# A two-block transformer kernel on one core: the high by high terms of each stage's first product are issued ahead of the terms with low parts

## What is computed

```python
def rmsnorm(a, g):
    af = a.astype(jnp.float32)
    af = af * lax.rsqrt(jnp.mean(af * af, axis=-1, keepdims=True) + EPS)
    return (af * g.astype(jnp.float32)).astype(a.dtype)
...
        h = rmsnorm(x, g_mix[i])
        z = h @ w_in[i]
...
        y = jnp.concatenate([rmsnorm(y_c, g_out_conv[i]), rmsnorm(y_a, g_out_attn[i])], axis=-1)
        x = x + y @ w_out[i]
        h = rmsnorm(x, g_ffn[i])
        gate = causal_dwconv3(h @ w_gate[i], ffn_conv_w[i], ffn_conv_b[i])
        x = x + (jax.nn.silu(gate) * (h @ w_up[i])) @ w_down[i]
        ple_gate = jax.nn.sigmoid(rmsnorm(x, g_ple[i]) @ w_ple_gate[i])
        x = x + ple_gate * (p[i].astype(x.dtype) @ w_ple_proj[i])
```

## Time and profile before

| | |
|---|---|
| median of three runs | 2513.19 us (2512.89 to 2514.77) |
| the profiled execution's own time | 2514.26 us |
| its span, first to last instruction | 2512.9 us |
| TensorE's matmuls busy | 2459.4 us, 98%, 11970 of them |
| VectorE, ScalarE, GpSimd busy | 1691.4, 1153.4 and 1469.0 us (67%, 46%, 58%) |
| mean granted TensorE clock | 0.999 |

### The profile page before, as it was taken

The page is one execution under the profiler, slowest core; times in us unless marked ns, Lnnn a source line. Parts: engine busy times, 40 slices in busy tenths (PEclk is TensorE's granted clock), DMA queues, the critical chain, the costliest instruction groups (busy, mean ns, idle before and its releaser), DMA issues.

```text
span 2512.9 us, 35613 instructions
## 1 busy us (share of the span) xinstructions
PE 2459.4 (98%) x11970; PEld 2039.0 (81%) x11970; DVE 1691.4 (67%) x2889; ACT 1153.4 (46%) x2207; POOL 1469.0 (58%) x1157
## 2 busy tenths in 40 slices
PE   8999999999999999999999999889999999999999
PEld 6888888887888888887877887679888888888887
DVE  5337776188988879997267888767238445445988
ACT  6336663253333335445256666586234333333442
POOL 2133324456777769997426555374346666667986
PEclk9999999999999999999999999999999999999999
DMA  4254323213322246332223122220321222227342
GB/s 160 76 182 129 114 77 130 105 59 118 114 100 101 106 168 222 118 95 88 91 74 91 61 70 80 89 85 22 151 76 63 107 108 101 101 97 267 118 159 97
DMA packets 125045, 274.67 MB, mean 109 GB/s; under 512 B 11809, under 2 KB 33601, under 8 KB 124609
## 3 DMA queue, kind: packets, MB, share of 16 engines
q1 hardware_dynamic: 124864, 272.40, 31.7%
HBM read 198.42 MB, written 69.21 MB: 107 GB/s over the span
## 4 chain that ended last, share of the span: by engine, by line
PE 83%; DVE 5%; POOL 5%; issue 4%; ACT 2%; DMA 1%; SPq 0%; DVEq 0%; ACTq 0%; POOLq 0%
PE PS L794 9%; PE PS L1056 9%; PE PS L1058 9%; PE PS L1057 9%; PE PS L796 9%; PE PS L795 9%; PE PS L1092 4%; PE PS L1093 4%; PE PS L1094 4%; PE PS L1347 2%; PE PS L928 1%; PE PS L899 1%; PE PS L1327 1%; POOL Wl L3564 1%; POOL RG L3670 1%
## 5 line engine op out<-in xcount | busy, mean ns | idle before, releaser
L794 PE MATMUL PS<-Hh,Wl 128*128 128x512 f32 x1072 | 433.8, 405 | 13.6 <-DVE Hl L1489 9.4
L796 PE MATMUL PS<-Hh,Wh 128*128 128x512 f32 x1072 | 420.5, 392 | 0.0
L795 PE MATMUL PS<-Hl,Wh 128*128 128x512 f32 x1072 | 419.9, 392 | 0.0
L3564 POOL TENSOR_TENSOR Wl<-Wr,Wh 128x512 fp32r<-128x512 f32 (+1 forms) x158 | 210.1, 1351 | 331.7 <-ACT Wh L2600 331.5
L3670 POOL TENSOR_TENSOR RG<-SW,RG 128x512 fp32r<-128x512 f32 x120 | 184.1, 1534 | 212.2 <-ACT RG L2928 199.3
L3670 POOL TENSOR_TENSOR RG<-RW,RG 128x512 fp32r<-128x512 f32 x176 | 258.2, 1477 | 64.7 <-ACT RG L2928 63.5
L1058 PE MATMUL PS<-Hh,RG 128*128 128x512 f32 x640 | 249.0, 389 | 0.0
L1056 PE MATMUL PS<-Hh,RG 128*128 128x512 f32 x640 | 249.0, 389 | 0.0
L1057 PE MATMUL PS<-Hl,RG 128*128 128x512 f32 x640 | 249.0, 389 | 0.0
L794 PEld LDWEIGHTS PS<-Hh,Wl 128*128 128x128 f32 x1072 | 204.4, 191 | 52.9 <-POOL Wl L3564 11.2
L796 PEld LDWEIGHTS PS<-Hh,Wh 128*128 128x128 f32 x1072 | 202.2, 189 | 44.6
(11 more groups left out here) (449 smaller groups left out, 6064.4 us busy)
## 6 DMA issues: line engine op xcount, KB each, us to landing
hgscr<-GB SPq DMA_DIRECT2D x98, 256.0 KB, 2.0
RW<-in_wg SPq DMA_DIRECT2D x44, 512.0 KB, 3.7
RW<-in_wu SPq DMA_DIRECT2D x44, 512.0 KB, 4.6
R<-in_wd SPq DMA_DIRECT2D x40, 512.0 KB, 3.8
Wr<-in_wi SPq DMA_DIRECT2D x27, 512.0 KB, 3.5
Hl<-hgscr SPq DMA_DIRECT2D x16, 768.0 KB, 7.1
hgscr<-acc SPq DMA_DIRECT2D x36, 256.0 KB, 2.0
HC<-hgscr SPq DMA_DIRECT2D x12, 768.0 KB, 6.2
```

The lines of the kernel that those rows point to most:

```text
L794: pe.matmul(ps(b), k.Wl[:, s, wc], xh[:, kx, sl], start=kk == 0, stop=False)
L795: pe.matmul(ps(b), k.Wh[:, s, wc], xl[:, kx, sl], start=False, stop=False)
L796: i = pe.matmul(ps(b), k.Wh[:, s, wc], xh[:, kx, sl], start=False, stop=kk == nk - 1)
L3564: i = pool.tensor_tensor(k.Wl[:, s, c], k.Wr[:, s, c], k.Wh[:, s, c].bitcast(F32), ALU.subtract)
```

## The change

In three products and in both feed-forwards a pass of high by high matmuls over all slices is issued first, each behind the high part of its slice; then the slices follow again with the two terms that have a low part. At the start, in the ple gate and in the two feed-forwards all eight slices go ahead, so 16 matmuls; in the first out-projection, whose order of slices is 4 to 7 and then 0 to 3, only the four attention slices, so 8 matmuls. The slots keep their places behind the slices of the second pass. The three products are the calls of `product` for mix, for the first out-projection (through `out_projection`) and for ple.

```diff
-    def product(parts, nk, half, slots=(), pace=3, order=None, fresh=None):
+    def product(parts, nk, half, slots=(), pace=3, order=None, fresh=None, high=None):
 
         slots = dict(slots)
         banks = [bank.next() for _ in parts]
+        ahead = [kx for kx in order or range(nk) if high and high(kx, half)]
+        for kx in ahead:
+            for e in high(kx, half):
+                pe.wait_ge(*at(*e))
+            for (u, (xh, _), _, _), b in zip(parts, banks):
+                if kx == ahead[0]:
+                    take(b)
+                    pe.wait_ge(*at("w_hi", u))
+                pe.matmul(ps(b), k.Wh[:, slot_of(u), 128 * kx:128 * kx + 128], xh[:, kx, half_of(half)], start=kx == ahead[0],
+                          stop=False)
...
-                pe.matmul(ps(b), k.Wl[:, s, wc], xh[:, kx, sl], start=kk == 0, stop=False)
-                pe.matmul(ps(b), k.Wh[:, s, wc], xl[:, kx, sl], start=False, stop=False)
-                i = pe.matmul(ps(b), k.Wh[:, s, wc], xh[:, kx, sl], start=False, stop=kk == nk - 1)
+                pe.matmul(ps(b), k.Wl[:, s, wc], xh[:, kx, sl], start=kk == 0 and not ahead, stop=False)
+                i = pe.matmul(ps(b), k.Wh[:, s, wc], xl[:, kx, sl], start=False, stop=kx in ahead and kk == nk - 1)
+                if kx not in ahead:
+                    i = pe.matmul(ps(b), k.Wh[:, s, wc], xh[:, kx, sl], start=False, stop=kk == nk - 1)
...
+    def hi(tag):
+        return lambda kx, half: [("h_hi", tag, half, kx)]
...
-    product([(u0, H, ("qk", 0), False), (u1, H, ("qk", 1), False)], 8, 0, fresh=lo("mix"))
+    product([(u0, H, ("qk", 0), False), (u1, H, ("qk", 1), False)], 8, 0, fresh=lo("mix"), high=hi("mix"))
...
+    def high_y1(kx, half):
+        return [("y_hi", kx, half)] if kx >= 4 else []
...
             for half, f in ((0, 0), (0, 1), (1, 0), (1, 1)):
+                opens = (half, f) == (0, 0)
+                for step in range(8) if opens else ():
+                    pe.wait_ge(*at("h_hi", tag, 0, step))
+                    for z, n in enumerate((GU[f, 11], GU[f, 21]) if step < 4 else (GU[f, 12], GU[f, 22])):
+                        b = PLAIN[f][z][0]
+                        if step == 0:
+                            take(b)
+                        if step in (0, 4):
+                            pe.wait_ge(*at("g_hi", tag, n))
+                        wh = k.RG[:, RING[tag][n % 8], 0, 128 * (step % 4):128 * (step % 4) + 128]
+                        pe.matmul(ps(b), wh, k.Hh[:, step, half_of(0)], start=step == 0, stop=False)
...
-                        pe.matmul(ps(b), wl, xh, start=step == 0, stop=False)
-                        pe.matmul(ps(b), wh, xl, start=False, stop=False)
-                        i = pe.matmul(ps(b), wh, xh, start=False, stop=step == 7)
+                        pe.matmul(ps(b), wl, xh, start=step == 0 and not opens, stop=False)
+                        i = pe.matmul(ps(b), wh, xl, start=False, stop=opens and step == 7)
+                        if not opens:
+                            i = pe.matmul(ps(b), wh, xh, start=False, stop=step == 7)
...
-                    {5: lambda: stat("ple", 0), 7: lambda: stat("ple", 1)}, fresh=lo("ple"))
+                    {5: lambda: stat("ple", 0), 7: lambda: stat("ple", 1)}, fresh=lo("ple"), high=hi("ple"))
```

More of the change, by code:

```diff
@@ L784, in piece @@
                 if kk == 0:
-                    take(b)
+                    if not ahead:
+                        take(b)
                     if u not in loaded:
@@ L970, in tensor, with out_projection @@
                 bg.drain()
-    def out_projection(tag, fresh, slots):
+    def out_projection(tag, fresh, slots, high=None):
         u0, u1 = next(unit), next(unit)
         product([(u0, H, ("out", tag, 0, 0), False), (u1, H, ("out", tag, 1, 0), False)], 8, 0, slots, order=ORDER,
-                fresh=fresh)
+                fresh=fresh, high=high)
         us = {0: u0, 1: u1}
@@ L989, in fresh_y1 @@
         return [("h_lo", "conv", half, kx)]
-    out_projection("ffn", fresh_y1, {0: lambda: spread("conv", 0), 3: lambda: stat("conv", 1), 6: lambda: spread("conv", 1)})
+    def high_y1(kx, half):
+        return [("y_hi", kx, half)] if kx >= 4 else []
+    out_projection("ffn", fresh_y1, {0: lambda: spread("conv", 0), 3: lambda: stat("conv", 1), 6: lambda: spread("conv", 1)},
+                   high_y1)
     def feed_forward(tag, nxt):
@@ L1019, in block_products @@
                         b = PLAIN[f][z][half]
-                        if step == 0:
+                        if step == 0 and not opens:
                             take(b)
```

## The result

The changed kernel took 2524.26 us (median of 5 runs, 2523.57 to 2527.11) against 2513.19 us (median of 5, 2512.15 to 2514.92): +11.07 us, ratio 1.0043 with a 95% interval of 1.0032 to 1.0053. Forecast were 2523.1 us, a range of 2519.0 to 2527.5, and a chance of 0.89 for slower.

What follows compares the result with a forecast made beforehand. TensorE, 83% of the chain, was taken to bound the kernel. Five openings sum to +8.55 us, plus 1.4 us for one clock fall: +9.95 on the 2513.19 us median gives 2523.1 us, range 2519.0 to 2527.5.

Steps and rivals of the forecast that it cites:

- The rival in which later waits on VectorE shrink: Three later waits on VectorE could shrink and take up the delay: +4.3 us, 2517.5 us; chance 0.08.
- The rival in which high parts come in time: Ple gate's high parts come in time, two waits vanish, start gains 0.9: -3.5 us, 2509.7 us; chance 0.03.
- Item 1: Program start: first matmul at 8.2 us instead of 9.38, waits of 0.75 and 0.9 us for high parts; -0.35 us.
- Item 2: First out-projection: the four attention slices' high parts are ready, no wait added; 0 us, ends 0 and +0.3.
- Item 3: First feed-forward: TensorE waits for late high parts, 2.6 us first; +4.2 us, ends +3.7 and +4.6.
- Item 4: Ple gate: two old waits go, TensorE idles 4.3 us for slices 6 and 7; +1.5 us, ends +1.1 and +1.8.
- Item 5: Second feed-forward: waits for late high parts as in the first, from another start; +3.2 us, ends +2.8 and +3.6.
- The clock: Openings where TensorE idles: the clock falls to half once, taken as 1.4 us, between 0 and 1.7.
- the rival with falls at two openings: Clock falls at two or three openings, 1.7 us each: 2525.1 to 2526.8 us; chance 0.20.

Runs made afterwards that it cites:

- the six-slice gate alone: Against the kernel before, only the ple gate changed: its first six slices go ahead, both statistics stand one product later; 2511.40 us, ratio 0.9992.
- the filler: Kernel with the pass in the ple gate only, plus 17 matmuls with unused results in the wait for slice 6; 2516.76 us, ratio 1.0011.
- the version with six slices: Against the kernel before: the start's pass, plus six slices ahead and later statistics in the ple gate; 2510.54 us, measured again 2509.60 us.

## Why the prediction was right, and where its numbers were off

**What bounds the kernel.** Right: the passes' waits went one for one into the time, none was taken up later. The rival in which later waits on VectorE shrink is refuted by the 2.7 us wait, still 2.7 to 2.8 us in every profile. The rival in which high parts come in time is refuted by the 2.39 us wait, the same whether TensorE reaches the opening at 506.3 or at 507.6.

**Item 1, the start.** Forecast -0.35 (ends -0.9 and +0.4). The 0.8 us by which the first norm's statistics came earlier (32.96 against 33.75) lie in that range, but the means over the five profiles with the pass and the seven without are 32.3 and 33.7, and the kernel with it alone measured -2.0. The first matmul was right (8.09 for 8.2). Two steps were not. The wait of 0.75 us for the second slice did not come, and the one for the fifth was 0.56 us for 0.9, since ScalarE's parts came earlier in the changed kernel:

```profile
8.52 1.99 ACT L2713 ACTIVATE Hh<-X,cols 128x512 fp32r<-128x512 f32 x3 [0.48 <-DMA X<-in_xT]
...
12.03 2.54 ACT L2713 ACTIVATE Hh<-X,cols 128x512 fp32r<-128x512 f32 x4
```

In the earlier trace rows these rows stand at 9.21 and 12.85, behind a DMA in both kernels. In the eleven profiles other than that one the second slice begins at 8.02 to 8.58, so the sum had taken one late transfer for the kernel's own. The other step held the slow pace to its place near 17.3. It is no fixed place: in the kernel with the start's pass alone it had ended by 12.39. Where it ended at about the same time, the pass is worth 0.7 to 0.8 us: the first norm's statistics stand at 32.67 in the second execution of the changed kernel against 33.34 in the six-slice gate alone (full pace at 16.8 in both), 32.96 against 33.75 in the changed kernel and before (17.2 and 17.4). The two profiles that gained more, at 30.93 and 31.44, are the two in which the slow pace ended early. Whether the pass makes that likelier is open, and with it how much of the 2.0 us is the pass's own.

**Item 2, the out-projection.** Right at 0: its pass of eight stands at 415.95 without a wait, and VectorE takes up the norm at 419.31 against 419.19.

**Item 3, the first feed-forward.** Forecast +4.2 (3.7 to 4.6), measured +4.7, +4.6. The first wait was right (2.39 for 2.6 us), and so was the hand calculation of the parts. Of the 0.9 us wait that the sum had before the sixth slice 0.20 was left, because the four matmuls ahead of it ran slowly (1.84 us; in the second execution they took 1.40 and the wait was 0.65). The error is in "with 0.5 us for a pair after a wait": the last pair ran at half clock, and the pass ended at 516.06 instead of 515.5. The granted clock is 0.50 from 513 to 515 and 1.00 again from 516. So 0.5 us of the item belong to the clock, and the item without it is the forecast 4.2.

**Item 4, the gate.** Forecast +1.5 (1.1 to 1.8), and the filler measured +1.7 without a low clock. The wait was 4.19 for 4.3 us.

**Item 5, the second feed-forward.** Forecast +3.2, measured +3.2 in both profiles of the kernel (15.10 and 15.09 against 11.92), with a clock of 1.00.

**The clock.** This is the term that was mis-sized. I took one fall for 1.4 us. In the profile of the changed kernel there were two at its openings: 3.4 us of half clock in the first feed-forward, which cost only 0.5 us since the rest lay under waits for high parts, and a longer one in the gate, worth 4.2 - 1.7 = 2.5 us. Together 3.0 us. The second profile has 6.6 - 4.2 = 2.4 and 3.7 - 1.7 = 2.0. So the rival with falls at two openings described what happened, and the price was nearer to the forecast's, as this rival's case against it said: much of the slow time lay under waits. Without the clock the items make 4.2 + 1.7 + 3.2 = 9.1 less 0.8 to 2 for the start, so 7.1 to 8.3; with 3.0 us it is 10.1 to 11.3. The measured 11.07 lies in that. That the forecast total is only 1.1 us off is in part luck: the clock took 1.6 us more than I had given it, and the start gave back half a microsecond or more beyond its own.

**A sentence that one execution had made.** I used the 1.00 in 621:631 of the earlier trace rows as evidence that the clock holds through 2.7 us. In eight of the twelve profiles it did not: seven to fourteen matmuls behind that wait were slow, at a cost of 1.6 to 2.8 us, in kernels whose feed-forward is that of before as well. One of them, of the second run of the version with six slices (same columns):

```profile
621.00:631.00 10.00, 7.29 (x26) 5.57 (x25) 8.76 (x11) 4.72 (x8) 6.78 (x6) 0.83 0.08 31
```

The 7.29 us of busy time and the wait are those of before; 26 matmuls began instead of 32. So the 1.6 us of this row in the table of stretches need no cause in the feed-forward's pass. Whether the start's pass makes them likelier is open: they came in all five profiles with that pass and in three of seven without. The Trainium skill, TensorE: Matmul & The Clock Gate, section "Why this matters for your kernels", asks for no idle gap longer than some microseconds. By the first profile the 2.7 us gap agreed with it; over twelve profiles it went either way, and behind the 4.2 us gap the clock fell in three of three. But it also fell in three of three behind the shorter 2.39 us wait of the first feed-forward, and once more where small matmuls had split that wait and no part of it was longer than 1.15 us. So the length of the longest gap alone does not tell here. The two other differences of the table are the executions' own: a fall of the clock near 1359 (after, and near 1349 in the kernel with filler and the gate with six slices alone) or between 1580 and 1590 (before, and both kernels with only the feed-forwards' passes, in full or three slices), and a wait of 2.2 us where the first down-projection begins, seen once in twelve. Before has a second low stretch, 0.83 in 1630 to 1640, that the changed kernel has in neither profile; with the one at 1580 it is what its row in the table, -1.2, is put down to. Nine of the twelve profiles have a fall there, behind waits of at most 1.7 us.

## What to carry to other kernels

Putting the terms whose operands come first at the head of a sum asks for the last of these operands sooner: a pass of 16 matmuls wants eight parts in 3.2 us, where the slice by slice order gave their producer 9.5. Compare that rate with the producer's rows before moving anything, and take ahead only as many terms as have their operands ready; in the gate, six slices ahead together with later statistics gained 1.6 us and eight slices lost 2.4; in the feed-forwards, three slices ahead changed nothing, as there was no wait to remove. An idle gap of TensorE is to be priced with the clock behind it, and what the clock did there is to be read from several profiles, not one. A first sum made from one profile also takes in that execution's late transfers.

## What the runs showed of the hardware that was not expected

**The slow pace at the start has no fixed length.** The first matmul at full pace came at 17.38 us in before, at 15.95 to 17.88 in the other kernels whose start is unchanged, and with the pass at 17.22 and by 16.8 (the changed kernel twice), by 12.4 (start alone), by 12.9 and at 18.26 (the version with six slices twice). The PEclk of the stretches reads 1.00 there all the time, so for the first microseconds the pace is read from the distance of the matmuls, 0.43 us against 0.227, or 0.28 to 0.34 where they wait for ScalarE's parts at full pace. The Trainium skill, TensorE: Matmul & The Clock Gate, section "What's actually happening", calls the number of slow matmuls at a start variable from run to run; these rows agree.

**One gap, different prices.** Behind the same 2.39 us wait in the first feed-forward the half clock ended at 516 in one profile of the changed kernel and after 518.01 in the other, 1.9 us of difference in the time of the stretch. Summed over the spans in stretches of 10 us, the clock's shortfall (10 us times one less PEclk) was 4.4 us in the profile of before and 9.1 and 11.0 in the two of the changed kernel, but also 11.7 in the one with only the feed-forwards' passes and 2.7 in the one with the six-slice gate alone. Each fall costs 1.6 us or more where no wait covers it, so a few of them would account for executions of one kernel that are up to 7 us apart; that they do was not measured run by run.
